# A gated delta rule and a sparse attention on one core: the mask moved to VectorE, the triangular inverse transposed once per level, and slots of the delta phase rearranged

## What is computed

```python
proj = h @ w_in[l]                      # h: 1024x1024, normed and modulated x
qkv = causal_dwconv_silu(concat([qa, ka, va]), conv_w[l])      # 4 taps
qa = l2norm(qa) * GDN_DK ** -0.5; ka = l2norm(ka)
# gated_delta_rule, per head and chunk of 64 tokens
gamma = exp(where(causal, decay_i - decay_j, -inf))
a_mat = where(strict, (kb @ k^T) * gamma, 0.0)
sol   = triangular_solve(a_mat + eye, [v * beta, kb * exp(decay)])
attn  = (q @ k^T) * gamma
def step(S, xs):                         # 16 chunks, one after another
    v_new = u_n - w_n @ S
    o = qg_n @ S + attn_n @ v_new
    S = S * exp(dl_n) + kd_n^T @ v_new
oa = rms_norm(oa, gdn_norm_g[l]) * silu(za);  ya = oa @ w_o_gdn[l]
# attention: per block of 128 queries and head
logits = q_lat @ ckv^T + bias            # -inf where a key isn't picked
o_lat  = softmax(logits) @ ckv;  yb = (o_lat @ w_uv * silu(zb)) @ w_o_dsa[l]
out = (sigmoid(ga) * ya + sigmoid(gb) * yb) @ w_out[l]
return rms_norm(x + gate * out, final_g)
```

## Time and profile before

| | before |
|---|---|
| time, median of 3 runs | 1651.97 us (1646.09 to 1652.5) |
| the profiled execution | 1650.57 us, its span in the trace 1648.7 us |
| PE busy | 1541.3 us, 93% of the span, 10038 instructions |
| DVE, ACT, POOL busy | 1019.9 us (62%), 526.8 us (32%), 506.1 us (31%) |
| granted TensorE clock, mean | 0.98 |

### The profile page before, as it was taken

The page is one execution under the profiler, slowest core; times in us unless marked ns, Lnnn a source line. Parts: engine busy times, 40 slices in busy tenths (PEclk is TensorE's granted clock), DMA queues, the critical chain, the costliest instruction groups (busy, mean ns, idle before and its releaser), DMA issues. The chain is left out here.

```text
span 1648.7 us, 27285 instructions
## 1 busy us (share of the span) xinstructions
PE 1541.3 (93%) x10038; PEld 957.1 (58%) x10038; DVE 1019.9 (62%) x1873; ACT 526.8 (32%) x1181; POOL 506.1 (31%) x543
## 2 busy tenths in 40 slices
PE   2899999999998999989898899999997999999997
PEld 2455884444444567757676676654443778864443
DVE  6629999999992455555555655434522666638333
ACT  2428321111112433543534334232101565531111
POOL 2420122222223543441431414123423333356000
PEclk9999999999999999999999999999998999999999
DMA  9100223323212222121210202236463000036122
GB/s 375 57 31 22 71 81 123 102 96 102 89 65 79 55 64 54 27 66 32 61 54 26 66 20 73 90 90 217 157 228 116 14 27 14 27 138 215 56 101 77
DMA packets 130876, 142.69 MB, mean 87 GB/s; under 512 B 17194, under 2 KB 104530, under 8 KB 128980
## 3 DMA queue, kind: packets, MB, share of 16 engines
q1 hardware_dynamic: 118676, 120.31, 23.2%
q10 hardware_dynamic: 12096, 20.98, 3.5%
HBM read 110.18 MB, written 31.08 MB: 86 GB/s over the span
## 5 line engine op out<-in xcount | busy, mean ns | idle before, releaser
L92 PE MATMUL ps<-g_h_hi,g_piece_hi 128*128 128x512 f16 x544 | 211.0, 388 | 4.3 <-PEq L1957 4.3
L93 PE MATMUL ps<-g_h_lo,g_piece_hi 128*128 128x512 f16 x544 | 210.0, 386 | 0.0
L94 PE MATMUL ps<-g_h_hi,g_piece_lo 128*128 128x512 f16 x544 | 209.7, 385 | 0.0
L92 PE MATMUL ps<-g_h_hi,a_w_hi 128*128 128x512 f16 x448 | 171.1, 382 | 6.9 <-DVE g_h_lo L523 5.2
L93 PE MATMUL ps<-g_h_lo,a_w_hi 128*128 128x512 f16 x448 | 171.1, 382 | 0.0
L94 PE MATMUL ps<-g_h_hi,a_w_lo 128*128 128x512 f16 x448 | 170.9, 382 | 0.0
L613 DVE MATCH_REPLACE8 a_ada<-a_best,a_ada 128x1024 f32<-128x1024 f32 (+2 forms) x192 | 166.6, 875 | 0.0
L610 DVE MAX8 a_best<-a_ada 128x8 f32<-128x1024 f32 (+2 forms) x192 | 160.9, 880 | 0.7 <-DVE a_ada L599 0.3
L837 POOL CAST g_piece_hi<-g_piece 128x1024 f16<-128x1024 f32 x41 | 47.9, 1169 | 343.8 <-PE ps L94 204.7
L239 POOL CAST a_w_hi<-a_w 128x2048 f16<-128x2048 f32 x14 | 26.5, 1891 | 273.8 <-PE ps L94 273.8
L1066 DVE SCALAR_TENSOR_TENSOR g_yq<-e_raw,g_taps,g_yq 128x1024 f32<-128x1024 f32 x60 | 90.7, 1512 | 28.6 <-ACT g_yq L913 26.5
(11 more groups left out here) (316 smaller groups left out, 3623.7 us busy)
## 6 DMA issues: line engine op xcount, KB each, us to landing
a_w<-in_w_in SPq DMA_DIRECT2D x18, 1024.0 KB, 5.7
g_piece<-in_w_in SPq DMA_DIRECT2D x34, 512.0 KB, 4.3
channel_gates<-a_x ACTq DMA_DIRECT2D x48, 256.0 KB, 2.0
e_lb<-diagonal_blocks SPq DMA_DIRECT2D x32, 256.0 KB
a_ada<-in_w_ada ACTq DMA_DIRECT2D x4, 1024.0 KB, 10.6
a_ada<-in_w_ada SPq DMA_DIRECT2D x4, 1024.0 KB, 15.8
a_x<-in_x SPq DMA_DIRECT2D x8, 512.0 KB, 20.8
delta_gate<-a_x ACTq DMA_DIRECT2D x32, 128.0 KB, 1.8
```

Source lines behind the costliest of these rows:

```text
L92: pe.matmul(out, a_hi, b_hi, start=first, stop=False)
L93: pe.matmul(out, a_hi, b_lo, start=False, stop=False)
L94: return pe.matmul(out, a_lo, b_hi, start=False, stop=last)
```

## The change

Three things are edited.

1. **The inverse, transposed per level.** `outer16` and `outer32` keep one product of the two. `turn_base` runs three times for each head, before each `middle`, and ScalarE copies b1 three times. VectorE's updates of b1 are gone. The chain begins earlier: `expand` at u = 27 (31 before), `turn_base` at 28, 34, 40, `middle` at 30, 36, 42, `outer` at 32, 38, 44. x32 is now the buffer x16, which VectorE clears in part at u = 46, and the gate's values no longer wait for the inverse.
2. **The slots.** `turn_q` moves from u = 28 to 30, `scores` from 30 to 32, `decay` from 8 to 10, the gating from 96 and 97 to 97 and 98, `turn_out` from 98 to 100. On VectorE and ScalarE the recurrence of all heads now comes first in a slot, and the other pieces in a second loop over the heads.
3. **The mask.** The mask's matmuls are gone. One VectorE instruction (`tensor_tensor_reduce`) adds the mask to the logits, writes the negated sum to SBUF (p), and takes its minimum; ScalarE exponentiates p in place. ORDER goes from (7, 0, 6, 1, 5, 2, 4, 3) to (0, 7, 1, 6, 2, 5, 3, 4).

```diff
-        x32 = zb[:]
+        x32 = x16
@@ SP
-                sp.wait_ge(tx64, min(h + 3, H))
                 sp.dma_start(zb[:], g.z_dram[...]).then_inc(z_in, 16)
...
-                if slot % SLOTS == 20 and 0 <= (slot - 92) // SLOTS < H:
+                if slot % SLOTS == 3 and 0 <= (slot - 75) // SLOTS < H:
@@ ScalarE
+                for h in heads(slot):
+                    u = slot - SLOTS * h
...
-                    if u == 32:
-                        act.wait_ge(bt, h + 1)
+                    if u in (28, 34, 40):
+                        act.wait_ge(bt, 3 * h + (u - 28) // 6 + 1)
                         nc.scalar.copy(b1, ...).then_inc(b1_ok, 1)
@@ VectorE
                         advance(h, e // 3)
+                for h in heads(slot):
+                    u = slot - SLOTS * h
...
-                    if u in (96, 97):
+                    if u in (97, 98):
...
-                            nc.vector.tensor_tensor(b1[odd, :, even], b1[odd, :, even], short(3)[odd, :, cols], ALU.subtract)
-                            nc.vector.tensor_tensor(t2[even, h % 3, :, odd], t2[even, h % 3, :, odd], short(2)[even, :, cols], ALU.subtract)
+                            nc.vector.tensor_tensor(t2[even, h % 3, :, odd], t2[even, h % 3, :, odd], short(3)[even, :, cols], ALU.subtract)
...
-                    if u == 31:
+                    if u == 27:
                         expand(h)
@@ TensorE
             def outer16(h):
                 pe.wait_ge(x16_ok, h + 1)
                 for i in range(NT):
-                    mm(half_at(3, i), t2[:, h % 3, i], columns(x16[:, i], 16, 0), start=True, stop=True)
-                for i in range(NT):
-                    last = mm(half_at(2, i), x16[:, i], columns(t2[:, h % 3, i], 16, 1), start=True, stop=True)
+                    last = mm(half_at(3, i), x16[:, i], columns(t2[:, h % 3, i], 16, 1), start=True, stop=True)
...
@@ attention, TensorE
-                    pe.wait_ge(exp_ok, n - 1)
+                    pe.wait_ge(top_ok, n - 1)
...
-                    last = mm(out, ident_b[:], mask[:, g.first[i] + c0:g.first[i] + c1], start=False, stop=True)
@@ attention, VectorE
+                if n >= 3:
+                    dve.wait_ge(turned, n - 2)
-                nc.vector.tensor_reduce(top[...], g.ps[:, at:at + wide[n]], AX.X, ALU.max, negate=True).then_inc(top_ok, 1)
+                nc.vector.tensor_tensor_reduce(out=p[:, n % 3, 0:wide[n]], in0=g.ps[:, at:at + wide[n]], in1=mask[:, c0:c0 + wide[n]], scale=-1.0,
+                                               scalar=-TAKEN, op0=ALU.add, op1=ALU.min, accum_out=top[...]).then_inc(top_ok, 1)
```

More of the change, by code:

```diff
@@ L708, in heads @@
         def heads(slot):
-            return [h for h in range(H) if 0 <= slot - SLOTS * h < 100]
+            return [h for h in range(H) if 0 <= slot - SLOTS * h < 102]
         def step_of(h, u):
@@ L1360, in scores, with turn_base @@
                 last.then_inc(qk, 1)
-            def turn_base(h):
-                pe.wait_ge(b2_ok, h + 1)
-                if h:
-                    pe.wait_ge(t_ok, h)
+            def turn_base(h, level):
+                if level == 0:
+                    pe.wait_ge(b2_ok, h + 1)
+                    if h:
+                        pe.wait_ge(t_ok, h)
+                elif level == 1:
+                    pe.wait_ge(up16, h + 1)
+                else:
+                    pe.wait_ge(up32, 2 * h + 2)
                 for i in range(NT):
@@ L1392, in outer32 @@
                 for i in range(NT):
-                    mm(half_at(3, i), t2[:, h % 3, i], columns(x32[:, i], 32, 0), start=True, stop=True)
-                for i in range(NT):
-                    last = mm(half_at(2, i), x32[:, i], columns(t2[:, h % 3, i], 32, 1), start=True, stop=True)
+                    last = mm(half_at(3, i), x32[:, i], columns(t2[:, h % 3, i], 32, 1), start=True, stop=True)
                 last.then_inc(tx32, 1)
             def middle64(h):
-                pe.wait_ge(up32, 4 * h + 4)
+                pe.wait_ge(b1_ok, 3 * h + 3)
                 for i in range(NT):
@@ L1768, in logits @@
                     out = g.ps[:, at + c0:at + c1]
-                    three(nc.tensor, out, q_hi[:, h, tok], q_lo[:, h, tok], k_hi[:, h % 2, c0:c1], k_lo[:, h % 2, c0:c1], True, False)
                     n0, n1 = max(c0, (i - 1) * P, 0), min(c1, (i + 1) * P)
-                    if n0 < n1:
+                    near = n0 < n1
+                    last = three(nc.tensor, out, q_hi[:, h, tok], q_lo[:, h, tok], k_hi[:, h % 2, c0:c1], k_lo[:, h % 2, c0:c1], True, not near)
+                    if near:
                         b0 = n0 - (i - 1) * P
-                        for part in (bias_hi, bias_lo):
-                            mm(g.ps[:, at + n0:at + n1], flip_h[:], part[:, h, b0:b0 + n1 - n0], start=False, stop=False)
-                    last = mm(out, ident_b[:], mask[:, g.first[i] + c0:g.first[i] + c1], start=False, stop=True)
+                        mm(g.ps[:, at + n0:at + n1], flip_h[:], bias_hi[:, h, b0:b0 + n1 - n0], start=False, stop=False)
+                        last = mm(g.ps[:, at + n0:at + n1], flip_h[:], bias_lo[:, h, b0:b0 + n1 - n0], start=False, stop=True)
                 last.then_inc(logit, 1)
@@ L1875, in peak @@
                     dve.wait_ge(exp_ok, n - 3)
-                at = scores_at(n)
-                nc.vector.tensor_reduce(top[:, n % 4:n % 4 + 1], g.ps[:, at:at + wide[n]], AX.X, ALU.max, negate=True).then_inc(top_ok, 1)
+                if n >= 3:
+                    dve.wait_ge(turned, n - 2)
+                at, c0 = scores_at(n), g.first[steps[n][1]]
+                nc.vector.tensor_tensor_reduce(out=p[:, n % 3, 0:wide[n]], in0=g.ps[:, at:at + wide[n]], in1=mask[:, c0:c0 + wide[n]], scale=-1.0,
+                                               scalar=-TAKEN, op0=ALU.add, op1=ALU.min, accum_out=top[:, n % 4:n % 4 + 1]).then_inc(top_ok, 1)
             def norm(n):
```

92 lines of the change are left out of this document (44 added, 48 removed).

## The result

The changed kernel takes 1622.79 us (median of 4 runs, 1620.01 to 1624.66), the kernel before 1651.51 (4 runs). The ratio is 0.9831, with a 95% interval of 0.9805 to 0.9857: 28.7 us faster. The profiled execution has a span of 1621.5 us, 27.2 less than before. The forecast was 1643, with a saving of 8.6 us in its sum. The saving is over three times that, and the time lies only 0.8 us inside the lower end of the range (1622), next to the faster rival (1626).

A forecast was written before the change was run, and what follows sets the result against it. TensorE, busy 93%, was taken to bound the kernel. The terms, -14.6 + 5 - 13.9 + 14.9 (delta's waits) - 0.5 + 0.5 (small moves) = -8.6, gave 1642 from 1650.57, or 1643 against the median; range 1622 to 1662.

The forecast's parts named there:

- the faster rival: Delta phase: the five steady heads wait only 0.7 to 1.5 us, too short for the clock to fall; 1626, chance 0.25.
- The mask's columns, -14.6: Attention: dropping the mask matmuls frees 15.5 us of TensorE, less 0.9 us ahead of a wait on GpSimd.
- VectorE's instruction at no cost: Attention: the new mask instruction costs what the reduction it replaces did, 1225 ns for 1024.
- The half-rate rival: Attention: VectorE's new instruction makes two passes, 1.07 us more in a step of 1024; 1657, chance 0.08.
- The new ORDER, +5: Attention: pieces of the next head's keys fall in wide steps 7, 6, 5 and delay the row's maximum; +5 us.
- The matmuls of the inverse, -13.9: Delta phase, TensorE: two sets of products a head go, two transpositions come; -1.74 us a head, -13.9 for eight.
- Heads 0, 1, 2: Delta phase: TensorE waits 10.2, 5.5 and 3.8 us at turn_base; +7.4 for head 0, +9.3 for the others together.
- Heads 3 to 7, 24.5: Delta phase: TensorE waits 4.9 us a head, 24.5 for five, as expand meets GpSimd's spans, cast and subtraction.
- That the lead frees the recurrence: Delta phase: the recurrence, now first in a slot on VectorE, passes GpSimd freely; part of the faster rival.
- The clock, -0.5: Low clock behind TensorE's waits: +6 us from heads 0 to 2, -6.5 in the steady heads.

The follow-up runs named there:

- system_first: The changed kernel with `system` (u = 14, 15) put ahead of the other pieces of the heads on VectorE; 1618.53 us.
- gate_back2: The changed kernel with the gating back at 96 and 97, turn_out at 98, and what follows at 98 and 99; 1638.05 us.
- no_lead: The changed kernel with one loop over the heads again on VectorE and ScalarE, so the recurrence doesn't lead a slot; 1621.29 us.
- slots_alone: The kernel before with only the slots moved (gating, turn_out, turn_q, scores, decay); old inverse, single loop and attention kept; 1641.3 us.
- lead_slots2: The kernel before with the slots moved and the recurrence leading on VectorE and ScalarE; old inverse and attention kept; 1629.35 us.
- delta_alone: The changed kernel with the attention part undone (phase_attention and ORDER of the kernel before); 1626.91 us.

## Why the prediction was right, and where it was not

*The mask's columns, -14.6.* Right: 14.8 with the old ORDER.

*VectorE's instruction at no cost.* Right: 1223 ns for 1024 where the reduction took 1225, and 83 ns more to read the accumulator. The half-rate rival is out.

*The new ORDER, +5.* The sign was right, the size was low: 7.6 in the windows, 7.2 in the time.

*The matmuls of the inverse, -13.9.* The count of matmuls fell as worked out, by 224 in all: 96 of the mask, 128 net of the inverse. No run has this term by itself. What is left of the delta phase once waits and clock are taken off is 14.2 us, close to it.

*Heads 0, 1, 2.* Right within 0.7 us each: 10.2, 5.5, 3.8 against 9.56, 5.58, 3.53. Head 0's was worked out from the old end of expand, those of heads 1 and 2 from the length of the chain from products to expand against TensorE's way to turn_base.

*Heads 3 to 7, 24.5.* This is the step that failed: "I take 4.9, close to the old one, as today's waits show the lock to be the rule." Measured are 2.26 for head 3 and 25.0 - 9.56 - 5.58 - 3.53 - 2.26 = 4.1 for the other four, 6.3 in all, 18.2 less than I had. The prediction had both ends: expand ahead of spans (1 us) or held until the subtraction ends (6). In the profiled execution expand starts with the end of substitution, ahead of spans, and is held in no head. The upper end was wrong too: where expand did come behind spans (head 4 of system_first, heads 3 to 6 of gate_back2), it was held by spans and not until the subtraction's end, and TensorE waited 1.5 to 2.5 us. I carried over today's waits, in which the gating met GpSimd's burst, and did not ask whether it would still meet it. It doesn't, since the chain to the end of substitution grew by 3.1 to 5.5 us, where the prediction had 2.3 at `system` and nothing in substitution. With 6.3 in place of 24.5 the sum is 1624 to 1625, and 1622.8 was measured. So the faster rival came true, with its size (1.3 us a head against its 0.7 to 1.5) and its reason in part: that the burst moves it did not say. That the time stayed inside the stated range owes more to the width of the range than to the forecast.

*That the lead frees the recurrence.* The prediction had it in the faster rival. In the changed kernel it earns nothing (no_lead), in the kernel with the old inverse it earns 12 us (slots_alone to lead_slots2). Of these two kernels it matters in the one where the gating is held.

*The clock, -0.5.* It came to -3.1 in the delta phase (17.5 to 14.4) and +1.5 behind attention: the sum was near. Its parts had the right signs and were larger than forecast: some +8.6 in heads 0 to 2 (+6 in the prediction) and -9.6 in the steady ones (-6.5).

What stays open: why the clock fell behind attention, where the same wait of 2.4 us stands ahead of it in both kernels. It fell in delta_alone as well (0.59 over 1442 to 1446), which has the attention of before, so the new attention isn't needed for it. And what a chain that starts later would give was not tried.

## What to carry to other kernels

When a stall comes from two engines whose big operations meet on a shared resource, work out where they will meet after the change, each counted from the same event, before the old stall is carried over. Here a chain that began 2 us later ran into more of the other engine's operations, became 4 us longer, and its end passed the place where the stall had been. Work taken from the busiest engine may come with an earlier request for something that isn't ready: beside the same slots with the old inverse, 13.9 us of matmuls were bought with 6.7 us more of waits and 7.0 more at the low clock. Try the small parts of a change one by one, too: the new order of the blocks cost 7 us, and leaving `system` behind the update that the change had put ahead of it cost 4 to 5.

## What the runs showed of the hardware

While a tap of VectorE with two SBUF operands runs, a small operation of GpSimd that begins behind it is held until about its end. In the changed kernel the subtraction of 96 elements beside the tap of 1.28 us at 609.60 takes 1.48 us, and the one before it, of 104 elements, 0.39:

```profile
608.74 0.39 POOL L854 TENSOR_TENSOR e_tc<-e_tc,e_tmp 128x104 f32<-128x104 f32 x1
...
609.65 1.48 POOL L854 TENSOR_TENSOR e_tc<-e_tc,e_tmp 128x96 f32<-128x96 f32 x1
```
```profile
609.60 1.28 DVE L1068 SCALAR_TENSOR_TENSOR g_yq<-e_raw,g_taps,g_yq 128x1024 f32<-128x1024 f32 x1 [1.97 <-ACT g_yq L912]
```

The hold goes both ways: whichever starts first runs at its own speed. Ahead of spans, expand takes 1.23 us and spans 2.90; behind it, in gate_back2, spans takes 1.91 and expand up to 2.50. That is what the Trainium skill says ("SBUF — State Buffer", Who interferes with whom: the shared pair is an exclusive lock), and these rows agree. In the substitution, a chain of 30 small operations, each tap of VectorE that falls into it lengthens the chain by about a microsecond: it takes 11.8 us with none (heads 4 and 6 before the change) and 14.3 to 14.7 with three (heads 3 to 7 of the changed kernel).
